# Two transformer blocks on one core: modulations of the first norm as TensorE rows, x loaded first, a head's step moved into the fourth recurrence round

## The reference

```python
mod = c @ ada_w + ada_b                       # c: 1 x 1024, ada_w: 1024 x 6144
sh1, sc1, gt1, sh2, sc2, gt2 = split(mod, 6)
h = rmsnorm(x, norm1_g) * (1 + sc1) + sh1
xr, yr, q, k, v, ga, gb = split(h @ w_in)     # w_in: 1024 x 7168
xr = causal_dwconv(xr, conv_w, conv_b)        # 4 taps
y_a = rg_lru(xr, ...) * gelu(yr)              # gated recurrence along the tokens
q, k = head_rmsnorm(q), head_rmsnorm(k)       # 8 heads of 128
y_b = stick_breaking_attention(q, k, v)       # softplus, suffix sums, exp
mix = sigmoid(ga) * y_a + sigmoid(gb) * y_b
x = x + gt1 * (mix @ w_out)
h2 = rmsnorm(x, norm2_g) * (1 + sc2) + sh2
x = x + gt2 * ((gelu(g_ff) * v_ff) @ ffn_down)  # g_ff, v_ff: 3-tap convolution of h2 @ ffn_up
```

## Time and profile before

| | us |
|---|---|
| median of 3 runs | 1749.9 (1748.2 to 1752.79) |
| the profiled execution | 1751.07 |
| its span | 1749.3 |
| PE busy | 1606.8 (92%) |
| DVE busy | 621.3 (36%) |
| ACT busy | 347.8 (20%) |
| DMA, mean | 312 GB/s, 545.46 MB |

### The profile page before, as it was taken

How to read it: one execution, slowest core, us unless ns; L and a number is a source line. 1 busy time by engine, 2 the same in 40 slices (tenths; PEclk the granted TensorE clock), 3 DMA queues, 4 the chain that set the end, 5 groups by cost and what they waited for, 6 DMA issues and landing times. The chain is left out here.

```text
span 1749.3 us, 20505 instructions
## 1 busy us (share of the span) xinstructions
PE 1606.8 (92%) x7270; PEld 888.5 (51%) x7270; DVE 621.3 (36%) x1434; ACT 347.8 (20%) x644; POOL 0.2 (0%) x4
## 2 busy tenths in 40 slices
PE   1999899999999887879999988989999999999986
PEld 1888787788888764733333322323333333333322
DVE  5557762589820377141212211211122112211112
ACT  1125563333210125131111110101011011111101
POOL 0000000000000000000000000000000000000000
PEclk8999899999999999878999999999999999999999
DMA  9836673457973330218999999999999999999994
GB/s 399 347 123 249 260 293 133 150 211 293 368 276 123 121 120 25 97 53 356 420 420 420 420 420 421 419 421 418 417 420 396 371 380 420 419 421 420 420 420 194
DMA packets 77220, 545.46 MB, mean 312 GB/s; under 512 B 8944, under 2 KB 9456, under 8 KB 11536
## 3 DMA queue, kind: packets, MB, share of 16 engines
q1 hardware_dynamic: 75760, 540.74, 76.3%
q10 hardware_dynamic: 1312, 2.75, 0.4%
HBM read 542.41 MB, written 1.05 MB: 311 GB/s over the span
## 5 line engine op out<-in xcount | busy, mean ns | idle before, releaser
L904 PE MATMUL bank<-ring,scr 128*64 128x512 f32 x2048 | 456.2, 598 | 19.0 <-DMA ring<-in_w_mlp 18.9
L507 PE MATMUL bank<-hT,ring 128*128 128x256 f32 x1856 | 415.7, 385 | 24.5 <-ACT hT L1084 24.0
L507 PEld LDWEIGHTS bank<-hT,ring 128*128 128x128 f32 x1856 | 358.7, 194 | 79.5 <-issue 28.8
L904 PEld LDWEIGHTS bank<-ring,scr 128*64 128x64 f32 x2048 | 143.4, 138 | 314.3 <-issue 257.0
L937 PE MATMUL bank<-ring,hT 128*64 128x512 f32 x1024 | 233.9, 597 | 2.2 <-DMA ring<-in_w_mlp 2.2
L2117 DVE TENSOR_SCALAR scr<-bank 128x256 f32<-128x256 f32 x64 | 27.0, 421 | 396.7 <-PE bank L904 396.7
L937 PEld LDWEIGHTS bank<-ring,hT 128*64 128x64 f32 x1024 | 68.5, 136 | 141.0 <-issue 130.9
L2187 DVE COPY hT<-bank 64x512 f32<-64x512 f32 x32 | 22.2, 695 | 315.3 <-PE bank L937 285.7
L1373 ACT ACTIVATE scr<-scr 128x256 f32<-128x256 f32 x64 | 26.7, 417 | 504.2 <-DVE scr L2117 504.2
L1490 DVE SCALAR_TENSOR_TENSOR ring<-ring,cb 128x1024 f32<-128x1024 f32 x96 | 113.3, 1219 | 9.5 <-DMA cb<-in_cb 6.0
L652 PE MATMUL bank<-scr,ring 128*128 128x256 f32 x384 | 83.5, 379 | 1.6 <-ACT scr L1229 1.6
(11 more groups left out here) (365 smaller groups left out, 1288.1 us busy)
## 6 DMA issues: line engine op xcount, KB each, us to landing
ring<-in_w_mlp SPq DMA_DIRECT2D x384, 1024.0 KB, 22.6
ring<-in_w_in SPq DMA_DIRECT2D x28, 1024.0 KB, 20.9
ring<-in_ada_w SPq DMA_DIRECT2D x24, 1024.0 KB, 8.3
ring<-in_up SPq DMA_DIRECT2D x24, 1024.0 KB, 5.7
ring<-in_w_ada SPq DMA_DIRECT2D x24, 1024.0 KB, 7.7
ring<-in_down SPq DMA_DIRECT2D x12, 1024.0 KB, 14.1
ring<-in_w2in SPq DMA_DIRECT2D x6, 1024.0 KB, 9.6
ring<-in_w_out SPq DMA_DIRECT2D x4, 1024.0 KB, 7.9
```

The costliest lines, as they stand in the source:

```text
L507: ins = mm(b[:, 256 * j:256 * j + 256], v[:, k * 256 + j * 128:k * 256 + j * 128 + 128], rhs[:, k, :], start=(k == 0), stop=(k == 7))
L904: ins = mm(HID[0][n][64 * hf:64 * hf + 64, :], K.xe[0][x % 2][:, xo:xo + 64], v[:, o0:o0 + 512], start=False, stop=(k == 7), skip_group_ch ...
```

## The change

- x is the first transfer of SyncE's list; cb and the large constants follow the eight first modulation pieces. ScalarE's queue keeps the small constants and the columns, in that order; c is added to the columns (8 of them).
- The eight pieces of the first modulation hold 128 rows of ada_w each, untransposed, 2048 columns ("ada0"). TensorE multiplies each with a column of c, broadcast to 32 columns, in four products: each gives 32 equal rows in its own 32 partitions of bank 5. ScalarE copies the bank (`rows`), TensorE transposes it into bank 6, VectorE picks one column of each 32 (16 for every block of 128), adds the bias, and makes the gains. VectorE's coefficient work for the gates now stands ahead of that. ScalarE loads the table of the root ahead of everything and squares x before it works on lam.
- Of the other modulations of the first block VectorE makes two a round of the recurrence instead of three, two behind ga 0, one behind each of ga 1 to 3 and one behind each of gb 0 to 2. The list has the same order.
- In the fourth round TensorE goes on to the gate products and ga 0 before the sums of head 3; ScalarE's `gates` and VectorE's `recurrence` are cut in two, and step 7 stands between the halves. All later steps come one place earlier; gb 2 and gb 3 have a step behind each of their halves. VectorE mixes pairs 0 to 2 between the steps and only pair 3 at the end.
- SyncE waits for the stores behind the loop instead of inside it.
- Two semaphores for the new steps; f_sq and f_tr are given up, and sq and h4_tr count on in their place.

```diff
@@ lay_pieces
             plan.append((("rg", c), a["rg"][c], 512))
-            for i in range(3 * c, 3 * c + 3):
-                ada(1 + i // 8, [i % 8])
+            ada(1, [2 * c, 2 * c + 1])
         for c in range(4):
             w_in(("ga", c), 20 + c)
-            ada(2, [4 + c])
+            ada(2, [[0, 1], [2], [3], [4]][c])
         for c in range(4):
             w_in(("gb", c), 24 + c)
+            if c < 3:
+                ada(2, [5 + c])
@@ sync_program
+    e.dma_start(K.xT[:, :, :], a["xT"]).then_inc(S.ld_x, 16)
     for i, (key, src, n) in enumerate(K.plan):
...
         if key == ("ada", 0, 7):
+            e.dma_start(K.cb[:, :], a["cb"]).then_inc(S.ld_cb, 16)
             e.dma_start(K.con[:, 256:NCONST], a["consts"][:, 256:NCONST]).then_inc(S.ld_con2, 16)
...
-            e.wait_ge(S.out, 64)
             e.wait_ge(S.m_left, 8)
+    e.wait_ge(S.out, 64)
@@ tensor_program
         norm_sum(0, c, K.sq1[c])
+    for k in range(8):
+        v = landed(("ada", 0, k))
+        for j in range(4):
+            ins = mm(B[5][32 * j:32 * j + 32, :], K.C("c", k).to_broadcast([128, 32]), v[:, 512 * j:512 * j + 512],
+                     start=(k == 0), stop=(k == 7))
+        ins.then_inc(S.piece_done, 1)
+    e.wait_ge(S.ada_row, 1)
+    for q in range(4):
+        ins = e.transpose(B[6][:, q * 128:(q + 1) * 128], K.rows[:, q * 128:(q + 1) * 128], ident)
+    ins.then_inc(S.ada_tr, 1)
     e.wait_ge(S.ld_con2, 16)
...
         if c < 3:
             chunk(("conv", c + 1))
-        att_step(2 * c + 1)
+            att_step(2 * c + 1)
...
     for c in range(4):
         chunk(("ga", c))
-        att_step(8 + c)
+        att_step(7 + c)
     for c in range(4):
-        chunk(("gb", c))
-        att_step(12 + c)
-    att_step(16)
+        if c < 2:
+            chunk(("gb", c))
+            att_step(11 + c)
+            continue
+        v, b = main(("gb", c))
+        for j in range(2):
+            for k in range(8):
+                ins = mm(b[:, 256 * j:256 * j + 256], v[:, k * 256 + j * 128:k * 256 + j * 128 + 128], K.hT[:, k, :],
+                         start=(k == 0), stop=(k == 7))
+            if j:
+                ins.then_inc(S.piece_done, 1)
+            att_step(9 + 2 * c + j)
@@ scalar_program
-    e.dma_start(K.cb[:, :], a["cb"]).then_inc(S.ld_cb, 16)
+    e.dma_start(K.con[:, 0:256], a["consts"][:, 0:256]).then_inc(S.ld_col, 16)
     e.dma_start(K.col[:, :], a["cols"]).then_inc(S.ld_col, 16)
...
+    e.wait_ge(S.consts, 3)
+    table(ACT.Sqrt)
+    e.wait_ge(S.ld_x, 16)
+    for c in range(4):
+        act(K.sq1[c], K.pair(K.xT, c), ACT.Square).then_inc(S.sq, 1)
+    norm_root(0, K.rst1)
...
+    landed(("ada", 0, 7))
+    act(K.rows, B[5][:, :], ACT.Copy).then_inc(S.ada_row, 1)
     modulate(0, 0)
...
-        att_step(2 * c + 1)
-        gates(c)
+            att_step(2 * c + 1)
+        gates_first(c)
+        if c == 3:
+            att_step(7)
+        gates_last(c)
     for c in range(4):
-        att_step(8 + c)
+        if c:
+            att_step(7 + c)
         landed(("ga", c))
...
-        att_step(12 + c)
+        att_step((11, 12, 13, 15)[c])
+        if c == 2:
+            att_step(14)
         landed(("gb", c))
@@ vector_program (after the coefficients)
+    e.wait_ge(S.ada_tr, 1)
+    columns = K.modc[:, 0, 0:16]
+    src = B[6][:, :].rearrange("p (b j r) -> p b j r", b=4, r=32)[:, :, :, 0]
+    e.tensor_copy(columns.rearrange("p (j b) -> p b j", b=4), src).then_inc(S.vec, done.one())
+    e.wait_ge(S.vec, done.n)
+    tt_(columns, columns, C("ada_b", 0, 16), ALU.add).then_inc(S.mod, 1)
+    e.wait_ge(S.mod, 1)
+    gains(0)
+    e.wait_ge(S.ld_cb, 16)
...
-        ada(1 + 3 * c // 8, 3 * c % 8)
-        att_step(2 * c + 1)
-        ada(1 + (3 * c + 1) // 8, (3 * c + 1) % 8)
-        recurrence(c)
-        ada(1 + (3 * c + 2) // 8, (3 * c + 2) % 8)
+        ada(1, 2 * c)
+        if c < 3:
+            att_step(2 * c + 1)
+            ada(1, 2 * c + 1)
+        recurrence_first(c)
+        if c == 3:
+            att_step(7)
+            ada(1, 7)
+        recurrence_last(c)
...
-        ada(2, 4 + c)
...
+        if c == 0:
+            ada(2, 0)
+        ada(2, c + 1)
...
+    for c in range(3):
+        att_step(11 + c)
+        ada(2, 5 + c)
+        if c == 2:
+            att_step(14)
+        mixed(c)
+    ada_bias(0, 1, 3)
+    att_step(15)
+    att_step(16)
+    mixed(3)
```

More of the change, by code:

```diff
@@ L35, in _layout_cols @@
     n = 0
-    for name, w in (("ada_b", 48), ("b_ada2", 48), ("norm1", 8), ("norm2", 8),
+    for name, w in (("c", 8), ("ada_b", 48), ("b_ada2", 48), ("norm1", 8), ("norm2", 8),
                     ("conv_w", 32), ("conv_b", 8), ("ba", 8), ("bx", 8), ("lam", 8), ("qg", 1), ("kg", 1),
@@ L105 @@
 sq nsum norm_rt rstd gain hn h x
-piece_done cb ada_use mod
+piece_done ada_row ada_tr cb ada_use mod
 qk_raw qk_sq qk_sum qk_rt qk
@@ L115 @@
 lg_cp lg_tr h4_tr h4 gz ge mk pos_mm pos gtn gt_tr gt_t
-f_sq f_acc f_tr
+f_acc
 ld_cb ld_col ld_x ld_con2 ld_pos ld_b2 out
@@ L198, in lay_scratch @@
         self.rst1 = carve(256)
+        self.rows = carve(512)
         place[0] = 0
@@ L275, in ada @@
             for k in parts:
-                plan.append((("ada", n, k), (a["ada_w"], a["w_ada_2"])[n // 3][n % 3, k], SLOT))
+                w = (a["ada_w"], a["w_ada_2"])[n // 3][n % 3, k] if n else a["ada0"][k]
+                plan.append((("ada", n, k), w, SLOT))
         def w_in(key, ci):
@@ L323, in lay_pieces @@
         for key, _, _ in plan:
-            if key[0] not in ("b1", "ada"):
+            if key[0] not in ("b1", "ada") or key[:2] == ("ada", 0):
                 n += 1
@@ L429, in sync_program @@
                 e.wait_ge(S.b1h, before[1] + 1)
-            elif before[0] == "ada":
-                e.wait_ge(S.ada_use, 8 * before[1] + before[2] + 1)
+            elif before[0] == "ada" and before[1]:
+                e.wait_ge(S.ada_use, 8 * before[1] + before[2] - 7)
             else:
@@ L1095, in scalar_program @@
     act(K.lt[0], K.lt[0], ACT.Exp, scale=-1.0).then_inc(S.coef, 1)
-    e.wait_ge(S.ld_x, 16)
-    for c in range(4):
-        act(K.sq1[c], K.pair(K.xT, c), ACT.Square).then_inc(S.sq, 1)
-    e.wait_ge(S.consts, 3)
-    norm_root(0, K.rst1)
+    landed(("ada", 0, 7))
+    act(K.rows, B[5][:, :], ACT.Copy).then_inc(S.ada_row, 1)
     modulate(0, 0)
@@ L1150, in conv_copy, with gates_first @@
             ACT.Copy).then_inc(S.xp_cp, 1)
-    def gates(c):
+    def gates_first(c):
         landed(("rg", c))
@@ L1163, in gates, with gates_last @@
         ins.then_inc(S.rg_th, 1)
+    def gates_last(c):
         e.wait_ge(S.rg_sig, c + 1)
@@ L1502, in vector_program @@
     e.memset(K.halfpi[:, :], np.pi / 2).then_inc(S.consts, 1)
-    e.wait_ge(S.ld_cb, 16)
-    for k in range(4):
-        ada(0, k)
     norm_end(0, K.rst1)
@@ L1509, in vector_program @@
         tt_(K.hT[:, k, :], K.xT[:, k, :], K.rst1, ALU.mult).then_inc(S.hn, 1)
-    for k in range(4, 8):
-        ada(0, k)
-    ada_bias(0, 0, 1)
-    e.wait_ge(S.mod, 1)
-    e.wait_ge(S.ld_col, 32)
-    gains(0)
     lt = K.lt
@@ L1615, in att_step, with recurrence_first @@
             att_first(n // 2)
-    def recurrence(c):
-        W, mix = K.Wt, K.pair(K.mix, c)
+    def recurrence_first(c):
+        W = K.Wt
         e.wait_ge(S.rg_th, c + 1)
@@ L1621, in recurrence, with recurrence_last @@
         ts_(W[2], W[2], 0.5, 0.5, ALU.mult, ALU.add).then_inc(S.rg_sig, 1)
+    def recurrence_last(c):
+        W, mix = K.Wt, K.pair(K.mix, c)
         e.wait_ge(S.rg_ae, c + 1)
@@ L1657, in vector_program, with mixed @@
         tt_(mix, mix, K.Wt[2 + c % 2], ALU.mult).then_inc(S.mixga, 1)
-        ada(2, 4 + c)
-    ada_bias(0, 1, 3)
-    for c in range(4):
-        att_step(12 + c)
-    att_step(16)
-    for c in range(4):
+        if c == 0:
+            ada(2, 0)
+        ada(2, c + 1)
+    def mixed(c):
         mix, w = K.pair(K.mix, c), K.Wt[4 + c]
@@ L2220, in vector_program @@
             taken(0, 0).then_inc(S.f_acc, 1)
-            e.wait_ge(S.f_sq, 1)
+            e.wait_ge(S.sq, 21)
             taken(0, 1)
@@ L2225, in vector_program @@
             total(0)
-            e.wait_ge(S.f_sq, 3)
+            e.wait_ge(S.sq, 23)
             taken(1, 1)
@@ L2232, in vector_program @@
             for c in range(4):
-                e.wait_ge(S.f_tr, c + 1)
+                e.wait_ge(S.h4_tr, 4 + c + 1)
                 for j in range(2):
@@ L2266, in lay_out @@
     o["xT"] = np.ascontiguousarray(np_("x")[0].T.reshape(8, 128, 256).transpose(1, 0, 2))
-    order = ["ada_b", "b_ada_2", "norm1_g", "norm2_g", "conv_w", "conv_b", "rg_ba", "rg_bx", "rg_lambda",
+    order = ["c", "ada_b", "b_ada_2", "norm1_g", "norm2_g", "conv_w", "conv_b", "rg_ba", "rg_bx", "rg_lambda",
              "q_norm_g", "k_norm_g", "ffn_conv_w", "ffn_conv_b", "g_pre_mix_2", "g_post_mix_2", "g_pre_ffn_2",
```

16 lines of the change are left out of this document (8 added, 8 removed).

## The result

| | before | after |
|---|---|---|
| median, us | 1753.22 (1748.2 to 1755.62, 6 runs) | 1737.57 (1733.29 to 1743.02, 6 runs) |
| ratio | | 0.9917 (95%: 0.9891 to 0.9943) |
| profiled execution, its span | 1751.07, 1749.3 | 1743.02, 1741.2 |

The change is faster by 15.65 us, 0.8% by the ratio; I had forecast 1729.4, within 1725 to 1737. The time lies 0.57 us above the range. Runs of before, of all sessions together, have a median of 1751.2 (44 runs of the three later groups), those of after 1737.1 (18 runs): 14.1 us by this larger count, of 20.5 forecast. Each against the runs of before in its own group, the three groups of the changed kernel give 15.65, 13.0 and 18.6 us.

What follows compares the result with a forecast made beforehand. It took the last 950 us to be bound by the experts' weight stream at full DMA rate, started when TensorE frees ring slots. Start 11.0, fourth round 6.2 and exit 3.3 sum to 20.5 saved: 1729.4 us, range 1725 to 1737.

Steps and rivals of the forecast that it cites:

- The three idle places: TensorE idle before its first projection (16.80 us), in the fourth recurrence round (7.15) and before w_out (some 4).
- rivals A and B: Start: column groups don't overlap, 1741.9, 6%; or they don't and weight loads stand bare too, 1755.4, 3%.
- E: Exit: SyncE's way back to the loop's condition is not hidden, 1732.7; chance 6%.
- at 2.4 GHz the chunk takes 7.1, at 1.2 for its first 3 us 8.6: Start: time of TensorE's first projection chunk by clock, putting its copy at 39.0 or 40.5.
- rival C: Start: the bursts run at 1.2 GHz, so it saves 10, 1730.4; 75% together with the forecast.
- I take 11.0: Start: first projection chunk's copy comes 11.0 us earlier, taken between 11.8 and 10.3.
- the 8 of the sum: Start: four transposes counted as 8 records of 128 columns, 0.9 us.
- I take 6.2: Fourth round: gain up to w_out's first result, between 7.2 and 5.5 with the clock drop.
- ga 0 at 224.0: Fourth round: ScalarE has ga 0 done at 224.0, after the recurrence ends at 223.4 (times of the old run).
- 3.4 us at half speed: Fourth round: if the clock falls in TensorE's 3.5 us wait before head 4's sums, this costs 1.7 us.
- Rival D: Fourth round gives nothing back: VectorE has more ahead of head 4, half-chunks stall more; 1735.6, 10%.
- A microsecond saved before the loop moves the whole stream a microsecond forward: Expert loop: time saved ahead of it shifts the full-rate weight stream of the last 950 us one for one.

Runs made afterwards that it cites:

- e3_exit: Kernel before with only SyncE's final wait for the stores moved behind the loop: 1748.14 us, ratio 0.9984.
- e9_all: Changed kernel with filler products at the start, large constants behind two projection pieces, and head 4's softplus step ahead of gate column 0's sigmoid and mixing: 1726.71 us.
- e8_early: Changed kernel with the large constants issued behind the first two projection pieces instead of ahead of them: 1734.97 us, ratio 0.9896.
- e7_warm: Changed kernel with unread filler products between the start's last modulation pieces and behind the transposes: 1738.15 us, ratio 0.9915.
- e5_order: Changed kernel with head 4's softplus step ahead of gate column 0's sigmoid and mixing on ScalarE and VectorE: 1728.98 us, ratio 0.9854.
- e6_later: Changed kernel with the second modulation behind gate column 0 done one column later, behind the head's step: 1732.03 us, ratio 0.9874.
- e12_after_again: Changed kernel run again with nothing edited, in the last group: 1735.07 us, ratio 0.9906.

## Why the prediction was wrong

**What bounds the kernel, rightly.** The three idle places and the exit were the right ones, all three gained; rivals A and B (column groups) are out with 1.06 us a piece, E with e3_exit.

**The start, right mechanism, term mis-sized.** 11.0 forecast, 9.1 in the trace, 8.65 by the medians. The step "at 2.4 GHz the chunk takes 7.1, at 1.2 for its first 3 us 8.6" failed: rival C was true, the bursts lost the clock (0.50 from 26.0 to 36.2), and the chunk took 9.2, 1.3 more than the 7.9 that "I take 11.0" leaves for it (50.84 - 11.0 - 31.9). The other 0.6 is the landing, at 32.5 instead of 31.9. At full clock, in e9_all, the chunk took 7.45 to its copy, so the half clock cost 1.75. The last piece (1.93) and the transposes (1.12) slowed down too, but after did not pay for that: in e8_early TensorE starts 0.75 us behind ScalarE's modulation, which for after gives 32.0, ahead of the landing. I had priced C at 10.0; that was 0.9 too much, 0.6 of it the landing. The transposes are 4 records, not the 8 of the sum; this changed nothing, for the same reason.

The Trainium skill describes products that wait for DMA between bursts and start cold ("TensorE: Matmul & The Clock Gate", "HAM oscillation — how this bites in real kernels"), in a case with longer waits than the 1.4 us here; the granted clock of 0.50 agrees with it. I gave it too little weight; alone it would have given 1730.4, so it is not the whole miss. The sentence of the Trainium skill in the section "The mechanism" of the same page, that a weight load is hidden only where its row group differs, is contradicted here: a piece took 1.06 us, not 2.0. What the clock cost could not be had back alone: e7_warm had the bursts at full clock, but its weights landed 0.8 us later and the clock fell behind the wait for them, so it won nothing.

**The fourth round, the failed step.** "I take 6.2": 5.0 in the trace and 3.4 by the medians. The wait was foreseen at its place, 3.5 us; it was 4.64. The term that failed is ScalarE's: "ga 0 at 224.0" has the sigmoid 0.6 us behind the recurrence and leaves out its table load, 1.28 us, which the trace has behind the recurrence's end and not beside it. (No run moved the load alone; e5_order and e6_later moved what stands around it.) VectorE's mixing waits for this sigmoid (2.00 us), and its two modulations and the head's step stand behind that, so all came 0.9 to 1.1 us late (times of the old run less 9.1: head step done 221.65, measured 222.53), the recurrence itself having ended 0.3 early. TensorE came to its wait 0.2 us early, which makes up the 4.64. The second term is the clock: not 1.7 but 2.5 us, (1.65 - 0.81) for the sums, 0.25 for their second part and (8.50 - 7.07) for gate column 3, where "3.4 us at half speed" were 6.8. Head 7's wait, 0.66 instead of 1.9, gave 1.2 back: 7.2 - 1.1 - 2.5 + 1.2 = 4.8, against 5.0 measured. Rival D ("VectorE has more ahead of head 4 than I count", 1735.6) came nearest, with the right place. e5_order shows what stood behind that wait: without it the round gives 11.1 us from first copy to output projection (242.1 before, 231.0).

**The scatter afterwards, not foreseen.** "A microsecond saved before the loop moves the whole stream a microsecond forward" holds in e12_after_again (12.8 us ahead at the output projection, 13.4 at the last stores), but only up to what the half clock does on the way: from one execution to the next 3 us ahead of the experts and 7 in them. This step failed for the profiled execution, which kept 4.9 us of its 14.1 up to the stores. By the medians the three groups give 13.0 to 18.6 against the traces' 17.3 (9.1 + 5.0 + 3.2), and all runs together 14.1. From the output projection to the experts the three traces of the old round take 485.6 to 486.6 us, of the eleven with the new one four take less and seven more; so part of the round's missing 1.6 us (5.0 and 3.4) may be a loss of the change, but three traces don't prove it. This stays open.

**The exit, right.** 3.3 forecast, 3.2 in the trace, 2.85 by the medians.

In sum: the medians of the parts miss the terms by 2.35, 2.8 and 0.45, which is 5.6 of the 20.5, and the whole missed by 4.85 in the first group, 7.5 in the second and 1.9 in the last. That 1737.57 lies only 0.57 above the range is in part the luck of the group. The range's upper end held D or E alone, not a smaller term at the start, one at the round and the scatter behind them at once.

## What to carry to other kernels

When a long wait before a short product is removed, look at what stands ahead of the next one on every engine that feeds it: here head 4's sums stood behind a sigmoid with a table load and two modulations, and swapping them on two engines was worth 5.0 to 6.1 us in the trace and 4.75 by medians beside after (7.9 over all runs), where the whole change had given 14.1. Where a start is bound by two things within a microsecond or two of each other (the landing and the chain of small steps, here), neither edit alone shows its worth; they must be tried together. Price a stall at its length plus the half clock that may come behind it: here 2.5 us behind 4.64, and between nothing and some 4 us behind one and the same stall of 2.28.

## What the runs showed of the hardware

Products with 32 columns of weights in four column groups ran four at once, 8 records of 512 columns in 1.06 us including the end of the last, with common row groups and loads of 0.13 us per four. Bursts of 1.06 us every 2.5 us dropped the granted clock to 0.50 after two of them; 6 filler records after each (1.56 us) kept it at 1.00, but in e7_warm it fell again, at 34, behind a wait of 2.60 us. A table load of ScalarE (1.28 us) began only when the wait ahead of its function had ended (214.08, behind 2.85 us). Two profiled executions of one kernel differed by 8.5 us in span with every instruction the same, and by 0.966 and 0.972 in mean granted clock; differences of 2 us and less between kernels need the marks in the traces and many runs, and even then the medians of three groups of the same kernel differ by up to 2.9 us.
